# A hybrid decoder step on one core: a new order of steps in the delta stage, and query sides of 232 and 312 columns in place of 272 and 272

## The reference

```
def gdn_chunk(S, q, k, v, g, beta):          # 4 heads, C tokens (here one chunk of 48, four of 128)
    G = cumsum(g);  decay = exp(where(incl, G_i - G_j, -inf))
    kb = k * beta
    L = where(strict, (kb @ k.T) * decay, 0.0)
    sol = triangular_solve(L, [v * beta, kb * exp(G)], unit_diagonal=True)
    u_v, w_k = sol[..., :dv], sol[..., dv:]
    v_new = u_v - w_k @ S
    attn = (q @ k.T) * decay
    o = (q * exp(G)) @ S + attn @ v_new
    S_new = S * exp(G_last) + (k * exp(G_last - G)).T @ v_new

def token_mixer(xn, ...):
    qkv, z, a, b, glu_in = split(xn @ w_in)
    q, k, v = heads(silu(causal_dwconv(qkv)));  q, k = l2norm(q), l2norm(k)
    o = rmsnorm(gdn(q, k, v, g(a), sigmoid(b))) * silu(z)
    c = silu(layernorm(causal_dwconv(glu(glu_in), 31 taps) + bias))
    return concat([o, c]) @ w_out

h = h + token_mixer(rmsnorm(h));  x = rmsnorm(h)
q = x @ w_query;  s = q @ sub_keys.T          # 8 heads x 2 sides x 128 keys
top 16 of each side, top 16 of the sums, softmax -> gates, expert numbers
h = h + sum over chosen experts of gate * gelu(x . u_e) * v_e
y = rmsnorm(h)
```

## Time and profile before

| | us |
|---|---|
| median of 3 runs (lowest to highest) | 1868.88 (1867.03 to 1873.43) |
| the profiled execution, its own time | 1871.53 |
| its span, first to last instruction | 1869.8 |
| PE busy in the span | 1798.9 |
| mean granted clock of PE | 0.975 |

### The profile page before, as it was taken

One profiled execution on the slowest core, in us unless ns is written; L12 is line 12 of the kernel. 1 busy time (PEld: TensorE's weight loads), 2 busy tenths in 40 slices (PEclk: granted clock), 3 DMA queues, 4 the chain that ended last, 5 costly groups with the idle time before them and its releaser, 6 DMA issues.

```text
span 1869.8 us, 29423 instructions
## 1 busy us (share of the span) xinstructions
PE 1798.9 (96%) x11505; PEld 1748.5 (94%) x11505; DVE 1383.7 (74%) x2531; ACT 715.1 (38%) x1252; POOL 673.4 (36%) x438
## 2 busy tenths in 40 slices
PE   7998988979899999999999999999999999999998
PEld 6997888769899999999999999999999999999997
DVE  4976887663599999999876566527778788888753
ACT  5545335442433343343343333333333333333342
POOL 3000000000001577768776776852344333333100
PEclk9988998879999999999999999999999999999999
DMA  7211001044302487989988999999999999999831
GB/s 212 77 38 46 32 9 44 23 107 148 105 25 91 163 285 264 301 292 312 307 303 290 311 322 314 308 343 358 331 384 381 348 340 354 355 342 344 313 116 37
DMA packets 190706, 424.33 MB, mean 227 GB/s; under 512 B 11162, under 2 KB 119222, under 8 KB 180320
## 3 DMA queue, kind: packets, MB, share of 16 engines
q1 hardware_dynamic: 153256, 287.47, 44.5%
q0 software_dynamic: 37312, 134.97, 20.5%
HBM read 360.76 MB, written 62.06 MB: 226 GB/s over the span
## 4 chain that ended last, share of the span: by engine, by line
PE 58%; DVE 16%; issue 2%; DMA 2%; POOL 1%; ACT 1%; DVEq 0%; POOLq 0%; ACTq 0%
PE psum L1296 29%; PE psum L1275 21%; PE psum L1263 3%; PE psum L902 3%; DVE junk L2424 2%; DMA act<-act_dram 2%; DVE besti L2287 1%; DVE sring L2291 1%; DVE besti L2299 1%; DVE best L2295 1%; DVE best L2283 1%; PE psum L907 1%; DVE WR L1793 1%; DVE oh L2414 1%; DVE eqx L2357 1%
## 5 line engine op out<-in xcount | busy, mean ns | idle before, releaser
L1275 PE MATMUL psum<-xT,WS 128*128 128x416 f32 x3072 | 594.7, 353 | 2.8 <-POOL WS L842 2.8
L1296 PE MATMUL psum<-AR,WS 128*128 128x416 f32 x3072 | 582.1, 351 | 4.6 <-DVE AR L2495 4.6
L1296 PEld LDWEIGHTS psum<-AR,WS 128*128 128x128 f32 x3072 | 575.4, 188 | 11.4 <-DVE AR L2495 5.3
L1275 PEld LDWEIGHTS psum<-xT,WS 128*128 128x128 f32 x3072 | 572.1, 188 | 8.5 <-POOL WS L842 4.0
L842 POOL TENSOR_TENSOR WS<-RAWP,WS 128x1024 fp32r<-128x1024 f32 x128 | 311.1, 2441 | 707.1 <-ACT WS L1693 610.0
L833 POOL DMA_INDIRECT rowg<-in_expert_v,idx x128 | 181.0, 1414 | 320.6 <-DVE acc L2438 312.8
L907 PE MATMUL psum<-xT,WR 128*128 128x280 f32 (+1 forms) x1968 | 276.0, 300 | 10.4 <-DVE xT L1820 7.2
L907 PEld LDWEIGHTS psum<-xT,WR 128*128 128x128 f32 x1968 | 264.4, 196 | 12.0 <-DVE xT L1820 7.8
L1703 ACT ACTIVATE WS<-RAWP 128x1024 fp32r<-128x1024 f32 x128 | 135.6, 1059 | 332.0 <-PE psum L1296 321.7
L2488 DVE TENSOR_TENSOR WS<-RAWP,WS 128x1024 fp32r<-128x1024 f32 x128 | 156.6, 1224 | 115.1 <-ACT WS L1703 115.1
L1730 ACT ACTIVATE actA<-psum 128x416 f32<-128x416 f32 x128 | 66.4, 519 | 401.5 <-PE psum L1275 395.2
(11 more groups left out here) (372 smaller groups left out, 1610.5 us busy)
## 6 DMA issues: line engine op xcount, KB each, us to landing
RAWP<-in_expert_u SPq DMA_DIRECT2D x64, 1024.0 KB
RAWP<-in_expert_v SPq DMA_DIRECT2D x64, 1024.0 KB
act_dram<-actA SPq DMA_DIRECT2D x128, 208.0 KB
gate_dram<-gblk SPq DMA_DIRECT2D x26, 1024.0 KB
act<-act_dram SPq DMA_DIRECT2D x64, 416.0 KB
Gt<-gate_dram SPq DMA_DIRECT2D x16, 1664.0 KB
RAW<-in_w_in SPq DMA_DIRECT2D x8, 1024.0 KB, 5.4
RAW<-in_w_query SPq DMA_DIRECT2D x8, 1024.0 KB, 8.3
```

The lines of the kernel that those rows point to most:

```text
L1275: last = mm(bank[e % 2][:, 0:TD], ws(e)[:, pw, kt * P:(kt + 1) * P], xT[:, px, kt, TSP:TPE], start=(kt == 0 and i == 0), stop=(kt == KT - ...
L1296: last = mm(bank[dt][:, 0:TD], ws(NK + e)[:, pw, dt * P:(dt + 1) * P], AR[:, e % 4, pa, :], start=(e == 0 and i == 0), stop=(e == NK - 1 a ...
```

## The change

Four things are changed. (1) The numbers of the list: FIRST of chunks 1, 2 and 4 is lower by 1.0, 2.6 and 1.2; `gb`, `k` and `ke` get places of their own per chunk (HEAD), earlier than before except in chunk 3; the steps of the outputs, the layer norm and the mixer's end are renumbered, some split (`lm` and `ln` by channel group, the conformer's low parts, the halves of the first three "out" units), and in all chunks but 3 ACT does `ke` before it copies `khT`. (2) The row sums of one column are issued in lots of 4, 3 and 3 between half units of their block, and no longer in one piece behind it. (3) The second norm: ACT's roots are no longer behind the next tile's square. (4) The query sides are 232 columns (the first two token tiles) and 312; the first query unit needs two normed tiles, not three.

```
+QSIDE = [(0, PT[2][0]), (PT[2][0], TPE - PT[2][0])]
...
-        FIRST = {0: 4.2, 1: 13.5, 2: 30.5, 3: 41.3, 4: 44.8}
+        FIRST = {0: 4.2, 1: 12.5, 2: 27.9, 3: 41.3, 4: 43.6}
+        HEAD = {"gb": {0: -2.4, 1: -2, 2: -2.4, 3: -1.2, 4: -2.4}, "k": {0: -1.3, 1: -0.8, 2: -0.7, 3: 0, 4: -0.8},
+                "ke": {0: -0.9, 1: -0.1, 2: -0.3, 3: 1.05, 4: -0.4}}
...
+            def row_sums(b, n, half):
+
+                lot = {(1, 1): (0, 4), (2, 0): (4, 7), (2, 1): (7, 10)}.get((n, half), (0, 0))
+                for x in range(*lot):
+                    c_, ci = 2 * (b - SC_QK) + x // len(CHUNKS), x % len(CHUNKS)
+                    if ci == 0:
                         A.wait(pe, "qk2", c_)
...
+                    c0, c = CHUNKS[ci]
+                    last = mm(bank[7][0:c, 8 * ci + c_:8 * ci + c_ + 1], sqb[c_ % 2][:, c0:c0 + c], ones[:, 0:1])
...
+            def inside_query(n, half):
+
+                if (n, half) == (0, 1):
+                    norm_tile(2, 3)
+                elif (n, half) == (1, 0):
+                    norm_tile(2, 4)
+                elif (n, half) == (1, 1):
                     V.wait(pe, "xlow", 2, NTP - 1, 1)
 
-            V.wait(pe, "xlow", 2, 2, 1)
+            V.wait(pe, "xlow", 2, 1, 1)
...
+            for t in range(2, NTP):
+                square(2, t)
+                root(2, t)
+                xhigh(2, t - 1)
+            xhigh(2, NTP - 1)
```

More of the change, by code:

```diff
@@ L1179, in first_out @@
                 b = first["out"]
-                for n in range(3):
-                    yield f"out{n}", MIX
-                    if n == 0:
-                        for i in (0, 1):
-                            for e, m, ci in held[i]:
-                                e.wait(pe, m, ci)
-                        V.wait(pe, "lm")
-                        V.wait(pe, "low", b)
-                    for half in range(2):
+                for half in range(2):
+                    for n in range(3):
+                        yield f"out{n}" + "ab"[half], MIX
+                        if half == n == 0:
+                            for i in (0, 1):
+                                for e, m, ci in held[i]:
+                                    e.wait(pe, m, ci)
+                            V.wait(pe, "lm")
+                            V.wait(pe, "low", b)
                         unit_half(b, UNIT0[b] + n, half)
@@ L1237, in _ @@
                 i = b - first["query"]
[L1238 removed]
+                if i == 0:
+                    linear(b, inside=inside_query)
+                else:
+                    linear(b)
                 score(2 * i)
@@ L1373, in evacuate_unit @@
                         T.wait(act, "score", ct - 2)
-                    fn(qT[:, ct % 2, half * PHALF:(half + 1) * PHALF], bk[:, 0:PHALF], ACT.Copy, "unit", u)
+                    c0, c = QSIDE[half]
+                    fn(qT[:, ct % 2, c0:c0 + c], bk[:, 0:c], ACT.Copy, "unit", u)
                 elif kind == "qkv":
@@ L2228, in mix_tile @@
             def mix_tile():
[L2230 to L2239 removed]
+                for k in range(HEADS, KT):
+                    yield f"cl{k - HEADS}", MIX
+                    if k == HEADS:
+                        A.wait(dve, "mixhigh", k, 0)
+                        op(tt(xT[:, 1, HEADS:, META:MIXED], cT[:, :, 0:TS],
+                              xT[:, 0, HEADS:, META:MIXED].bitcast(F32), ALU.subtract))
+                    mix_low(k, MIXED, NT, 0)
+                yield "high", MIX
+                low(first["out"])
+                yield "deltalow", MIX
+                A.wait(dve, "mixhigh", 0, 0)
+                op(tt(xT[:, 1, 0:HEADS, META:MIXED], qC[:, :, 0:TS],
+                      xT[:, 0, 0:HEADS, META:MIXED].bitcast(F32), ALU.subtract))
+                for k in range(HEADS):
+                    mix_low(k, MIXED, NT - P, 0)
                 dve.wait_ge(h_in, 48)
[L2241 to L2242 removed]
+                for t in range(2):
+                    yield f"out{t}b", MIX
                     add_out(first["out"], t)
@@ L2266, in _ @@
                     op(dve.memset(ss[:, 23:24], EPS), "ss0", 2)
-                for t in range(3 if b == first["out"] else 0, NTP):
+                for t in range(2 if b == first["out"] else 0, NTP):
                     add_out(b, t)
```

106 lines of the change are left out of this document (47 added, 59 removed).

## The result

The changed kernel takes 1860.05 us (median of 12, 1851.37 to 1865.13) beside 1869.16 us for the kernel before (12 runs, 1865.64 to 1873.89) on the same chip: ratio 0.9940, 95% interval 0.9926 to 0.9954. By the ratio it is faster by 11 us (the medians differ by 9) where I had forecast 27.5; 1860 lies in the outer part of my range, beyond my own 1832 to 1850. A second measurement of it, among the experiments, gave 0.9912 (0.9890 to 0.9935), 16 us; the two intervals overlap near 0.993, a gain of about 13 us. The profiled execution of the change took 1859.42 us, with a span of 1857.6.

The account below looks back on a forecast made before the run. PE bounds the kernel, 96% busy and solid from 502.3 us, so an earlier start of that run brings the end forward. Terms -1.5 - 5 - 4 - 7 - 3.5 - 6.5 = -27.5 us gave 1841 us, range 1823 to 1863.

Parts of the forecast that it names:

- row sums in lots: First stage: 5.1 us of half clock saved, a new 2.45 us wait, 1.1 given back: -1.5 us, between +2.5 and -3.
- the order (khT of chunks 0 to 2, dense part, end): Delta stage's new order: 0 for khT of chunk 0, -5 and -4 for chunks 1 and 2, -7 dense part, -3.5 end.
- dense part: 284 to 401.7 us: a fifth of 34 us idle or half clock won by the reshuffle, -7 us.
- start of the query blocks: First query unit needs only tile 1, so the scores start earlier, at 493.65 instead of 500.14 us: -6.5 us.
- price of 232 and 312 columns: Query MMs of 8 blocks: 109.3 and 145.8 ns by the slope, mean 127.6, no change: 0 us.
- khT of chunks 1 and 2: PE's waits of 3.48 and 4.49 us for KH go, with the half clock after them: -5 and -4 us.
- rival (b): DVE takes the place of the khT waits and the dense part gives nothing: 1857 us, chance 0.12.
- The end of the delta stage: ONB's wait only moves; 3.3 us of other waits and 0.9 of clock won, 0.7 lost: -3.5 us, between 0 and -9.
- The Trainium skill's rule: Clock gate follows how busy the engine was, so row sums in lots bring nothing and cost the wait: +2.45 us.
- rival (a): Query units of 232 columns run at the F32 price, 401 ns an MM: +112 us, 1953 us, chance 0.16.
- Rival (c): The order works better: half of the dense part's 34 us and all of both khT terms, -42, 1827 us, chance 0.09.
- (d): Nothing changes: the new 2.45 us wait and ONB set off further clock drops that eat the rest, 1866 us, chance 0.03.

Follow-up runs that it names:

- rows_only: The kernel before with the row sums in lots of 4, 3 and 3 alone: 1869.28 us, ratio 0.9995.
- ln_whole: Changed kernel with later row-sum lots, later chunk 4, late K, 272 columns after the first query block, and the layer norm in one piece again: 1850.03 us, ratio 0.9916.
- chunk4_late: The changed kernel with chunk 4 and the steps behind it 1.2 places later, as before: 1853.74 us, ratio 0.9922.
- q_only: The kernel before with the query part alone (sides of 232 and 312, two-tile wait, second norm's new order): 1856.28 us, ratio 0.9951.
- after_again: The changed kernel measured once more, nothing altered: 1854.20 us, ratio 0.9912.
- rows_late: The changed kernel with each lot of row sums one unit later in all blocks but the last: 1851.67 us, ratio 0.9913.
- q272_later: The changed kernel with 232 and 312 columns in the first query block alone, 272 and 272 in the other seven: 1854.30 us, ratio 0.9930.

## Why the prediction was wrong in its size

**The marks, over all profiles.** Row sums, by the start of khT of chunk 0: in one piece 148.08, 149.04, 152.31, 148.63 and 148.89 (mean 149.4), in the changed lots 151.00, 151.19, 151.84, 152.23, 148.71, 151.29 and 149.38 (150.8), in later lots 146.84, 146.58, 147.47, 146.17 and 146.67 (146.7). The order, from there to the keys' transposes: of before 317.6, 315.1 and 311.0 (mean 314.6); as changed 310.9, 310.9, 305.0, 310.9, 310.0, 307.0 and 303.8 (308.3). From xnS to the scores 29.94 and 30.19 without, 22.6 to 22.7 with the query part. From the scores to the experts 102.12 and 103.09. That makes +1.4 - 6.3 - 7.3 + 1.0 = **-11.2 us**, beside the 11 us of the first measurement. That they meet so closely is luck: the first two terms are differences of means of 3 to 7 single executions that spread over 4 to 7 us, and the second measurement gave 16.

| step of the prediction | forecast | measured |
|---|---|---|
| row sums in lots | -1.5 | +1.4 |
| the order (khT of chunks 0 to 2, dense part, end) | 0 - 5 - 4 - 7 - 3.5 = -19.5 | -6.3 |
| start of the query blocks | -6.5 | -7.3 |
| price of 232 and 312 columns | 0 | +1.0 |
| sum | -27.5 | -11.2 |

**The step that failed is khT of chunks 1 and 2, with the dense part.** I gave the two waits -9 us with their half clock. Both waits went, and the idle time of the stretch stayed: 14.5 and 14.8 us, and 14.6 with K back in its place. The clock of 0.95 behind the change is also that of rows_only with the old order. DVE delivers KH earlier (at 175.21 + 0.69 for chunk 1, from its timeline, where it was 178.91 + 0.68) and what it passes on the way later, so the next product that needs DVE or ACT waits. I had that as rival (b), and at 1857 us it came nearest of all cases; but DVE's own 13.4 us of slack was not the bound, since DVE was busy for only 78.66 of 94 us behind the change. The reading that fits is that a chain of steps through PE, ACT and DVE sets this stretch; the equal idle times bear it out, and no run shows the chain itself. The 7 us of the dense part were a fifth of what the one trace of before showed as idle or half clock. ln_whole shows no gain by the split of the layer norm in that stretch, and chunk4_late none by the earlier chunk 4. What the whole order did win in idle time can be read between the marks, from khT of chunk 0 to the keys' transposes; of before and q_only (old order), then of after and after_again:

```profile
148.08:465.63 317.55, 282.64 (x2001) 264.85 (x2001) 214.64 (x339) 132.79 (x335) 0.00 (x0) 0.89 0.20 58
149.04:460.07 311.03, 274.46 (x2000) 257.65 (x2001) 214.59 (x339) 132.65 (x335) 0.00 (x0) 0.91 0.21 59
151.00:461.86 310.86, 279.84 (x2001) 261.56 (x2002) 214.20 (x339) 131.62 (x334) 0.00 (x0) 0.91 0.21 59
151.84:461.80 309.96, 277.25 (x2001) 259.66 (x2001) 213.98 (x339) 131.63 (x334) 0.00 (x0) 0.92 0.21 60
```

PE is idle for 34.9 to 36.6 us in the three profiles with the old order and for 31.0 to 32.7 in the seven with the new one: 4 us less, beyond their spread, and it lies behind 285 us, as the stretch from 145 to 285 us shows none of it. The other 2 us of the 6.3 are busy time, which overlaps between the two orders (274.5 to 282.6 us and 272.6 to 279.9) as the half clock comes and goes.

From khT of chunk 0 to r3 of chunk 4 (the marks' first stretch without its end) the order of before took 248.9, 246.4 and 242.5 us in three profiles, the changed one 244.3, 244.3, 244.3, 242.1, 239.4, 237.4 and 237.1: means 245.9 and 241.3, so -4.6 us where I had -16. And the trace I forecast from was the longest of its three in this stretch, by 3.0 us above their mean.

**The row sums** went as the working said and one term short. The wait was forecast at 2.45 us and measured 2.37. The half clocks at 100 and 120.5 us went. I left out that the new wait could set off one of its own, as it did in the profiled execution: 10.2 us at half clock, 5.1 us lost, as much as was saved. In the profile that I had, the waits for KH of chunks 1 and 2 both had a low period with them, so it was there to be read. rows_late shows that the wait is needed for it: without the wait no low period there in any of five profiles. It is not sure to follow: five of seven profiles with the wait have it. Against the sums in one piece +1.4 us is a difference of means whose members overlap (148.1 to 152.3 and 148.7 to 152.2), so its sign is open. The Trainium skill's rule that I cited ("TensorE: Matmul & The Clock Gate", section "What's actually happening") would have given +2.45 us here, against my -1.5; +1.4 lies between. What I set against the rule, half clock with PE busy throughout, stands, and the change added 20.5 us of it at 298.5.

**The end of the delta stage**: 68.5 to 68.7 us in the profiles with the order of before, 67.1 on average with the changed one, -1.6 for -3.5. The profiles with the changed order that count here are those of the list above, 66.3 to 67.9 us. The wait at `on` of chunk 3 was said to move and cost the same; it is 0.6 us longer (4.38). The conformer's wait of 1.90 and VN's of 3.23 went, as forecast, and 1.18 us for xT stand at 417.31.

**The start of the query blocks** was right, -7.3 for -6.5, and q_only's 9.2 us in the whole agree with its counting in full at the end, as a solid run of PE behind it would have it.

**The columns**: rival (a), the F32 price, is refuted: 24 MMs of 232 columns take 477.10 - 474.34 = 2.76 us, 115 ns each, where that price had 401. The slope had 109.3, the floor 119.8; the truth is halfway. The cost over seven blocks was 0.97 us, 1.4 ns an MM, and q272_later gives it back.

Rival (c) fell with the dense part, and (d) is not what happened, though its mechanism, a new wait that sets off a clock drop, was real in the row sums.

**Open.** Which part of the order holds the 6 us. Of the three that were undone none costs anything measurable; left are the earlier chunks 1 and 2, the earlier `gb`, K of chunks 0 and 4, and the split of the first output block. Chunks 1 and 2 at their old places with the rest unchanged was not tried.

## What to carry to other kernels

A wait in a chain of dependent steps over three engines need not be a sum to be won: before counting it, name the next product that needs the delayed engine, and test by the idle time of the whole stretch, not by the wait's row. A wait of 2 us in a full run of TensorE cost here its own length in two profiles and about twice that in five, where half clock followed, and it was cheap to avoid: the instruction that waited could stand one unit later. And do not price a reshuffle from a share of one trace: here stretches of 240 us with the same instructions differed by 6 to 7 us between executions, so compare several profiles before a term of a few us is believed.

## What the runs showed of the hardware that I had not expected

- The granted clock fell behind a wait of 1.53 us and stayed low for a time that varied between executions of one order: 20.5, 17.1 and 6.8 us at the same products near 299 us. It did so with PE busy in all of the 20.50 us.
- Behind one and the same wait of 2.37 us the clock fell for 10.2 us in five profiles and did not fall in two.
- 32 instructions of plain F32 products of 8 columns in a row took 3.64 us at clock 1.00 in one kernel, and 6.83 us at 0.50 in another.
- F32R products cost 115 ns at 232 columns, between the slope from longer ones (109.3) and the 119.8 ns of 256 columns.
- The expert stages, with the same instructions, took 1257.1 to 1269.8 us from the first expert product to the span's end in the profiles of this study, 12.7 us apart, as much as the whole change is worth; one profile's total does not tell such changes apart.
